# The output projection of a hybrid decoder block as seven half-size products

## What is computed

```
y_ret = (silu(g) * head_norm(retention(q, k, v))) @ w_ret_o     # 2048 -> 1024
y_rnn = (rg_lru(conv(xr)) * gelu(gr)) @ w_rnn_o                 # 1024 -> 1024
mixed = sigmoid(m_ret) * y_ret + sigmoid(m_rnn) * y_rnn
x = x + mixed @ w_out                                           # 1024 -> 1024, the changed product
h = rms_norm(x, ffn_norm_g)
x = x + (silu(gate) * val) @ w_down                             # gate, val from conv(h @ w_up)
```

## Time and profile before

| | us |
|---|---|
| median of 3 runs | 1989.42 |
| lowest and highest | 1987.3, 1989.48 |
| profiled execution, first to last instruction | 1988.8 |
| PE busy in it | 1961.3 (99%) |
| DVE, ACT, POOL busy | 1418.8, 934.4, 333.9 |

### The profile page before, as it was taken

How to read it: one execution, slowest core, us unless ns; L and a number is a source line. 1 busy time by engine, 2 the same in 40 slices (tenths; PEclk the granted TensorE clock), 3 DMA queues, 4 the chain that set the end, 5 groups by cost and what they waited for, 6 DMA issues and landing times.

```text
span 1988.8 us, 24558 instructions
## 1 busy us (share of the span) xinstructions
PE 1961.3 (99%) x9208; PEld 1639.4 (82%) x9208; DVE 1418.8 (71%) x1621; ACT 934.4 (47%) x1182; POOL 333.9 (17%) x277
## 2 busy tenths in 40 slices
PE   8999999999999999999999999999999999999998
PEld 6888888888888888888888787997888888888887
DVE  7877876776755445667777658658987888776766
ACT  6443353343445555555555443346544544543335
POOL 2000010010392000067775003100000000000000
PEclk9999999999999999999999999999999999999999
DMA  6343554445697443465668555532222222256523
GB/s 259 117 169 137 180 181 157 169 158 179 206 327 281 159 159 127 148 200 173 206 190 256 199 196 194 184 112 84 85 91 78 84 84 84 74 191 234 199 96 132
DMA packets 222205, 325.07 MB, mean 163 GB/s; under 512 B 11824, under 2 KB 150448, under 8 KB 221872
## 3 DMA queue, kind: packets, MB, share of 16 engines
q1 hardware_dynamic: 196800, 232.84, 35.5%
q0 software_dynamic: 22608, 85.99, 11.0%
q10 hardware_dynamic: 2720, 5.24, 0.8%
HBM read 223.36 MB, written 100.66 MB: 163 GB/s over the span
## 4 chain that ended last, share of the span: by engine, by line
PE 83%; DVE 9%; ACT 3%; DMA 2%; issue 2%; POOL 1%; ACTq 0%; SPq 0%; DVEq 0%; POOLq 0%
PE ps L346 27%; PE ps L348 27%; PE ps L347 27%; DVE ws L329 1%; DMA stg<-scr_y 1%; DMA raw<-scr_q 1%; PE ps L1219 1%; POOL qkvs L949 1%; POOL state_s L955 1%; DVE ysr L2415 0%; DVE wx L2155 0%; POOL ws L968 0%; DVE wsr L2408 0%; ACT ri L1648 0%; DVE th L2337 0%
## 5 line engine op out<-in xcount | busy, mean ns | idle before, releaser
L1501 ACT ACTIVATE wx<-raw 128x1024 fp32r<-128x1024 f32 (+1 forms) x152 | 137.3, 905 | 252.3 <-DVE raw L2131 131.4
L346 PE MATMUL ps<-xs,wx 128*128 128x512 f32 x612 | 239.1, 391 | 2.1 <-DVE xs L2578 1.6
L348 PE MATMUL ps<-xs,wx 128*128 128x512 f32 x612 | 238.3, 389 | 0.0
L347 PE MATMUL ps<-xs,wx 128*128 128x512 f32 x612 | 238.2, 389 | 0.0
L2155 DVE TENSOR_TENSOR wx<-raw,wx 128x1024 fp32r<-128x1024 f32 (+1 forms) x152 | 158.9, 1047 | 30.4 <-ACT wx L1501 30.2
L346 PE MATMUL ps<-sc,wx 128*128 128x512 f32 x448 | 174.4, 389 | 0.0
L348 PE MATMUL ps<-sc,wx 128*128 128x512 f32 x448 | 174.3, 389 | 0.0
L347 PE MATMUL ps<-sc,wx 128*128 128x512 f32 x448 | 174.3, 389 | 0.0
L1536 ACT ACTIVATE ub<-ps 128x512 f32<-128x512 f32 x112 | 66.9, 597 | 159.1 <-PE ps L348 156.4
L346 PEld LDWEIGHTS ps<-xs,wx 128*128 128x128 f32 x612 | 114.9, 188 | 28.4 <-issue 2.7
L348 PEld LDWEIGHTS ps<-xs,wx 128*128 128x128 f32 x612 | 114.9, 188 | 24.1
(11 more groups left out here) (289 smaller groups left out, 4849.2 us busy)
## 6 DMA issues: line engine op xcount, KB each, us to landing
raw<-w_in SPq DMA_DIRECT2D x80, 512.0 KB, 5.5
scr<-ost POOLq DMA_DIRECT2D x32, 1024.0 KB, 5.2
raw<-w_up SPq DMA_DIRECT2D x44, 512.0 KB, 4.2
tq<-w_down SPq DMA_DIRECT2D x88, 128.0 KB, 2.7
scr_t<-tq POOLq DMA_DIRECT2D x22, 512.0 KB, 3.2
scr_h<-vt POOLq DMA_DIRECT2D x11, 1024.0 KB, 4.3
tr<-w_ret_o SPq DMA_DIRECT2D x64, 128.0 KB, 3.9
scr_q<-tr POOLq DMA_DIRECT2D x16, 512.0 KB, 5.2
```

The lines of the kernel that those rows point to most:

```text
L346: pe.matmul(out, w(HI), x(HI), start=first, stop=False, skip_group_check=True)
L347: pe.matmul(out, w(HI), x(LO), start=False, stop=False, skip_group_check=True)
L348: return pe.matmul(out, w(LO), x(HI), start=False, stop=last, skip_group_check=True)
L1501: act.activation(dst, src, ACT.Copy).then_inc(sem["f_hi"], 1)
```

## The change

The output projection becomes 14 chunks (28 to 41) of the kind of the retention projection: seven products of quarters, two chunks each, four token tiles of 6 matmuls of 512 columns in a chunk. The mixed pieces go unsplit into quarters `mq` (A11, A12, A22, A21); two more forms are made in place, S3 = A11 - A21 and S2 = A22 - S3 by DVE, A21 + A22 and A12 - S2 by POOL. The products are ordered so that they use PSUM banks 4 to 7 and 0 to 3 in turn. The sums of the weights are made by POOL, in eight pieces that SP loads during chunks 5 to 18 of the retention projection, and kept in `scr_o`. The transposes for token half 0 move to the last two chunks.

```
+O_W = ["b11", "b21", "t2", "t1", "t3", "b22", "t4"]
+O_BANK = [4, 0, 4, 0, 4, 0, 4]
+O_FORM = [Q_A11, Q_A12, Q_S2, Q_A21, Q_A11, Q_A12, Q_A22]
...
+            PIECES_AT = {5: (0,), 6: (1,), 7: (2,), 8: (3,), 11: (4,), 13: (5,), 17: (6,), 18: (7,)}
             for i in range(4, R_CHUNKS):
                 reto_w(i)
+                for j in PIECES_AT.get(i, ()):
+                    out_pieces(j)
...
+            def out_combine(j):
...
+                pool.tensor_tensor(tr[:, v, 0:2, :], tr[:, v, 0:2, :], tr[:, v, 1:3, :], ALU.subtract).then_inc(late_sem("tr_st"), 1)
...
+                pool.tensor_tensor(tr[:, v, 2, :], tr[:, v, 0, :], tr[:, v, 2, :], ALU.add).then_inc(late_sem("tr_st"), 1)
...
+                pool.tensor_tensor(tr[:, v, 3, :], tr[:, v, 3, :], tr[:, v, 2, :], ALU.subtract).then_inc(late_sem("tr_st"), 1)
...
+            for c in range(2):
+                k = slice(2 * c, 2 * c + 2)
+                pool.wait_ge(sem["o_s"], 2 * c + 1)
+                pool.tensor_tensor(mq[:, Q_A21, k, :], mq[:, Q_A21, k, :], mq[:, Q_A22, k, :], ALU.add).then_inc(sem["o_p"], 1)
...
-            for m in range(8):
-                pair, slot = out_block(m)
-                block_ready(pe, pair, slot)
...
+            def out(i, tiles=(0, 1, 2, 3)):
...
+                pe.wait_ge(*late_count("rw_lo", i + 1))
+                pe.wait_ge(*late_count("ry_lo", i + 1))
...
+            for i in range(R_CHUNKS, R_CHUNKS + 12):
+                out(i)
+            out(R_CHUNKS + 12)
+            pe.wait_ge(sem["xn_done"], 8)
+            pe.wait_ge(sem["x1_done"], 12)
+            for k in range(4):
+                turn2(k, 0, k)
+            out(R_CHUNKS + 13, (0, 1, 2))
+            for k in range(4, 8):
+                pe.wait_ge(*late_count("a11_in", k - 3))
+                turn2(k, 0, k - 4)
+            out(R_CHUNKS + 13, (3,))
...
-            def mixed_lo(n):
...
             def mixed(n):
+                half, t = mix_at(n)
                 dve.wait_ge(sem["mx_mul"], n + 1)
...
+            out_lo(i + 11)
+            out_add(5, 0, 1, 0)
+            out_lo(i + 12)
+            out_add(5, 0, 1, 1)
+            norm2(0)
+            norm2(1)
             norm2(2)
             norm2(3)
...
+            out_lo(i + 13)
             s_lo(A11, a11f, 0, 1)
             s_lo(A11, a11f, 1, 2)
-            out_add(6, 0)
+            prep_lo(0, 0, "b1")
+            combine_t4(0, 0)
+            out_last(0)
```

More of the change, by code:

```diff
@@ L986, in _ @@
             store_rnno(HEADS - 1)
+            for j in range(O_PIECES):
+                out_combine(j)
             for n in range(16):
@@ new lines, in out_free @@
+            def out_free(p, t):
+                if p == 0:
+                    pe.wait_ge(sem["acc"], 5 + t // 2)
+                elif p == 1:
+                    pe.wait_ge(sem["acc"], 7 + t)
+                else:
+                    pe.wait_ge(sem["x1_done"], (None, None, 1, 3, 5, 7, 9)[p] + t // 2)
+            def out(i, tiles=(0, 1, 2, 3)):
+                p, c, _ = out_at(i)
+                u = i % 2
+                pe.wait_ge(*late_count("rw_lo", i + 1))
+                pe.wait_ge(*late_count("ry_lo", i + 1))
+                for t in tiles:
+                    if c == 0:
+                        out_free(p, t)
+                    for k in range(2):
+                        last = mm3(pe, ps[:, O_BANK[p] + t, :], lambda q: ysr[u][:, q, k, t * P:(t + 1) * P],
+                                   lambda q: wsr[u][:, q, k, :], O_FIRST[p] and c == 0 and k == 0,
+                                   O_LAST[p] and c == 1 and k == 1)
+                    if c == 1:
+                        last.then_inc(sem["o_ps"], 1)
+                    elif t == 3:
+                        last.then_inc(late_sem("r_b"), 1)
@@ L1806, in norm2 @@
                 norm_scale_act(act, x1, t, sem["ss_done"], sem["std_done"], xn1, KT)
+            for i in range(R_CHUNKS, R_CHUNKS + O_CHUNKS):
+                reto_w_hi(i)
+                out_y_hi(i)
+                if i == R_CHUNKS:
+                    mixed_next(9)
+                elif i == R_CHUNKS + 13:
+                    for t in range(4):
+                        norm2(t)
             half_of = [None]
@@ L1837, in _ @@
             s_hi(A11, a11f, lambda c: act.wait_ge(*late_count("a11_in", 2 * c + 2)))
+            for k in range(4):
+                turned(4 + k + 1)
+                act.activation(a12f[:, k, :], ps[:, k, :], ACT.Copy, scale=gcol[4 + k]).then_inc(late_sem("a12_in"), 1)
             act.wait_ge(sem["x1_st"], 32)
@@ L1840, in _ @@
             act.wait_ge(fraw[0], 32)
[L1841 removed]
+            chunk_left(act, R_CHUNKS + 12)
             prep_hi(0, 0, "b1")
@@ new lines, in _ @@
+            reto_last(0)
+            reto_last(1)
+            mixed(10)
+            mixed(11)
+            reto_last(2)
+            reto_last(3)
+            mixed(12)
+            mixed(13)
+            out_lo(i + 1)
+            mixed(14)
+            mixed(15)
+            dve.tensor_scalar(neg_g[:, :], prm[:, PRM["ffn_g"]:PRM["ffn_g"] + KT], -1.0, None, ALU.mult).then_inc(
+                late_sem("neg_in"), 1)
+            out_lo(i + 2)
+            for c in range(2):
+                out_s3(c)
+                out_s2(c)
```

311 lines of the change are left out of this document (150 added, 161 removed).

## The result

The changed kernel takes 2011.2 us (median of 4 runs, 2007.4 to 2012.5) against 1989.1 us of the kernel before on the same chip (4 runs, 1987.3 to 1989.5). The ratio is 1.0107, with a 95% interval of 1.0093 to 1.0121. It is slower, as forecast, but by some 22 us where 14.5 were forecast, and 1.2 us above the upper end of the range. The profiled execution has a span of 2010.7 us against 1988.8; it belongs to the slowest of the four runs.

A forecast was written before the change was run, and what follows sets the result against it. The prediction took PE (TensorE) to bound the kernel, busy 99% of the span. Its terms, -17.6 - 4.5 + 6.5 + 7.6 + 8.0 + 3.8 + 5.6 + 5.1, gave +14.5 us, hence 2003.9 us, with a range of 1993 to 2010.

The forecast's parts named there:

- Matmuls: Output projection: 14 chunks of 5.44 us replace the 768 matmuls, -17.6 us.
- The start, and the pieces: Chunk 28 starts earlier without the splits, -4.5 us; w_out pieces shut DVE out in chunks 5 to 8, +6.5.
- Chunk 29 and its clock: PE waits for low parts behind late mixed pieces 12 and 13, +6.0 us, and the slow clock, +1.6.
- Chunk 31 and its clock: DVE's S3, S2 and low parts alternate with POOL's forms, +6.4 us, and the slow clock, +1.6.
- Chunks 40 and 41: Low parts come late behind an added result and the norms, +3.8 us.
- Into the FFN, first: The FFN's first product waits for a12f's copies and splits, +4.0 us, and the slow clock, +1.6.
- Into the FFN, second: The transposes wait for DVE's additions, norms and sums, +4.7 us, and the slow clock, +0.4.
- the row of 9.9 us: Profile row of a mix load landing in traffic, the upper bound for chunk 29's load, taken as 8.4 us.
- the walk: Waits followed forward from chunk 24 using the rows' durations; for chunk 29 it gave a PE wait of 6.0 us.
- everything lands late: Rival, chance 0.12: gates take 9.9 us, the clock drops longer, chunk 29 costs +9.4; 2007 to 2011 us.
- The port costs nothing: Rival, chance 0.1: DVE never waits for POOL, no waits at the pieces or chunk 31; faster, 1985.3 us.
- The pieces are hidden: Rival, chance 0.2: w_out pieces fit between DVE's operations or its idle time, without the 6.5 us; 1997.4 us.

The follow-up runs named there:

- forms_on_vector: The changed kernel with GpSimd's four operations on the mixed rows given to VectorE, behind the low parts of chunks 31 to 35: 2004.4 us, ratio 1.0081.
- pieces_11_18: The changed kernel with the eight pieces of w_out loaded and combined in chunks 11 to 18, one in each: 2010.4 us.
- end_order: The changed kernel with low parts, adds, norms, transposes and splits reordered behind chunk 39 alone: 2001.4 us, ratio 1.0059.
- x_later: The changed kernel with the second 2 MB reload of x issued behind chunk 33's weights instead of chunk 29's: 2005.9 us, ratio 1.0086.
- no_piece_sums: The changed kernel without GpSimd's 24 operations on the pieces of w_out, loads and stores kept, output not the reference's: 2005.5 us, ratio 1.0079.
- best_orders: The changed kernel with middle and end reordered, pieces in chunks 9 to 12 and 17 to 20, four GpSimd sums on VectorE: 1984.6 us, ratio 0.9968.
- best_orders_2: best_orders with the first reload of x behind chunk 31's weights and the t4 and t2 splits back between the last norms: 1984.9 us, ratio 0.9968.
- before_with_pieces: The kernel before plus the pieces' loads, GpSimd sums and stores in chunks 5 to 18, nothing reading them: 1997.6 us, ratio 1.0040.

## Why the prediction was right in kind and wrong in size

From the traces: PE starts the FFN's second block 21.85 us later than before (1375.63 against 1353.78), which is the whole difference of the spans. By the prediction's own steps:

| Step | forecast | measured | where it is read |
|---|---|---|---|
| Matmuls | -17.6 | -17.6 | chunks without a wait are 5.44 us apart |
| The start, and the pieces | +2.0 | 0.0 | from chunk 4, chunk 23 starts 5.3 us later than before, chunk 28 no later |
| Chunk 29 and its clock | +7.6 | +14.5 | chunks 29 and 30 start 17.26 and 8.13 behind the one before, instead of 5.44 |
| Chunk 31 and its clock | +8.0 | +6.3 | chunks 31 and 32: 9.06 and 8.10 instead of 5.44 |
| Chunks 40 and 41 | +3.8 | +4.0 | 6.51 and 10.06, where 5.44 and, with 16 transposes, 7.11 would do |
| Into the FFN, first | +5.6 | +5.8 | 11.52 from chunk 41 instead of 7.11, and 1.4 for two products, partly at the lower clock |
| Into the FFN, second | +5.1 | +7.1 | 5.0 to the transposes, and 24 transposes take 4.81 instead of 2.73 |
| Ahead of chunk 4, same code | 0 | +1.8 | chunk 4 starts at 1111.81 against 1110.00 |

A wait in this table is some 0.16 us longer than the idle time in the rows, since the last matmul ahead of it runs to its end. The measured terms add up to 21.9 us.

**The failed step is "Chunk 29".** Its mechanism held, its size did not: the wait was put at 6.0 us and measured 11.55, and 10.1 to 11.4 in the three runs that leave everything ahead of it nearly as it was (`forms_on_vector`, `pieces_11_18`, `end_order`). I took 8.4 us for the landing of the mix load beside the 2 MB reload and 9.9 as the bound, from a load that had landed in traffic before. It landed after 13.3 us. `x_later` shows that this is the reload's doing (5.1 us without it). What was misread is the row of 9.9 us. It is itself a load behind the second reload of `x`, as the issues of the kernel before show (the second line is the reload from issue to landing):

```profile
1239.32 0.37 SPq L785 DMA_DIRECT2D x<-x  x1
x<-x SPq DMA_DIRECT2D x1, 2048.0 KB, 11.4
1242.64 1.39 ACTq L491 DMA_DIRECT2D mrb<-scr_r  x1
```

and those of the changed kernel:

```profile
1244.32 0.37 SPq L842 DMA_DIRECT2D x<-x  x1
x<-x SPq DMA_DIRECT2D x1, 2048.0 KB, 12.7
1245.92 0.49 ACTq L512 DMA_DIRECT2D mrb<-scr_r  x1
```

In both, the load lands some 2 us behind the reload (1252.5 behind 1250.7, 1259.2 behind 1257.0). The kernel before issues it 3.3 us after the reload, the changed one 1.6 us, so it pays for more of the same 2 MB. Counted from the reload's issue, the row of before gives 13.2 us, hence 11.6 for a load issued 1.6 behind it: above the bound of 9.9, and still 1.7 short of the 13.3. With 13.3 in place of 8.4 the walk would have given 10.9 us. The rival "everything lands late", at 2007 to 2011, had the right idea and 0.12.

**The clock was priced too low for this execution.** I put 1.6 us behind each long wait, half of the 3.3 us in which the slow matmuls of before run. Behind the waits of chunks 29 and 31 the slow matmuls run for 5.2 us (12 of 512 columns, 0.427 apart), and 2.7 us are lost each time; 24 transposes behind the last wait lose 2.1 where I had 0.4. In all 3.7 us more than forecast. Part of this is the spread of executions: in the profile of `end_order` nearly the same two waits (11.37 and 4.51 us) lose 1.6 us each, as forecast.

**Chunk 31** waited less (3.46 against 6.4), since PE itself arrived late from chunk 29. The walk had the port right: low parts of 3.4 us in turn with GpSimd's, and no wait is left once GpSimd's operations are gone (`forms_on_vector`).

**The start and the pieces** were right in what they are. Chunk 23 starts 7.1 us later (1221.17 against 1214.07); less the 1.8 ahead of chunk 4, 5.3 are left for the pieces (forecast 6.5). From there to chunk 28 5.3 us come back (forecast 4.5), so chunk 28 starts 1.8 us later. Chunks 5, 6 and 7 start 6.7 us apart, the first 8.0 behind chunk 4, where 7.1 each were to be seen. That the pieces cost through the port is shown by `no_piece_sums`.

**The rivals.** "The port costs nothing" is refuted by two runs, which without GpSimd's operations were 5.7 and 6.8 us faster. "The pieces are hidden" is refuted by the rows of chunks 5 to 7. It would be true in chunks 9 to 12 and 17 to 20.

**Sums that do not come out.** Three operations of 1.30, 0.73 and 0.74 us are 2.8 us, not 2.6, which would have made the pieces' term larger and the miss there too. For chunk 29, a landing 1.5 us later makes the wait 7.5 us, not the 9.4 of the upper bound. In the rival without the port, the terms named (6.5, 2.0 of chunk 29 and 8.0 of chunk 31) are 16.5 and not 18.6. None of them changes the forecast's +14.5.

**Open.** Ahead of chunk 4 both programs run the same instructions. Chunk 4 started between 1109.7 and 1112.2 us in the 14 profiled executions of all versions, so I count the 1.8 us as the spread of executions; what causes it was not tried. Why the same waits lose 1.6 or 2.7 us to the clock is not known from these runs.

## What to carry to other kernels

Fewer matmuls are worth their time only in a stage where the next operand is ready; here 22.9 us went (17.6 of matmuls, 5.3 at the start) and some 43 us of waits and slow clock came, and 27 us of the result were had back by the order of work on the other engines and by giving four operations of GpSimd to VectorE. Before a load is priced, list what is issued in the microseconds around it on every queue, and ask the trace for a load behind the same megabytes, counting from the issue of these megabytes and not from its own; if there is none, the upper bound is open. And a GpSimd operation beside a busy VectorE costs VectorE its full length: give it to VectorE when that takes less time than it locks.

## What was new about the hardware

VectorE and GpSimd took turns, one instruction each, for as long as both had `tensor_tensor` work in SBUF: 1.22 us operations took 3.4 us, and GpSimd's 2.38 us ones 3.4 us too. The Trainium skill ("SBUF — State Buffer", Who interferes with whom) has the exclusive lock and lets whoever issues first have it; that neither engine went twice in a row in these stretches while the other had an operation ready is what the rows add.

The same wait did not always cost the same. At chunk 31, 3.46 us dropped the clock in the changed kernel and cost 2.7 us, while 3.63 us in `x_later` left it up; 2.95 us at chunk 30 of `best_orders` left it up, and 2.62 us at the same chunk of `best_orders_2` dropped it and cost 1.5 us. At chunk 5, 2.31 us left it up in the changed kernel and dropped it in `before_with_pieces`, but there the drop cost nothing: PE was ahead of VectorE, and what it lost at the lower clock came off its next waits. So a wait of 2 to 4 us should be priced with and without the drop, here 0 or 1.4 to 2.7 us, and the drop only where PE has no wait just behind it.
